# ScalarE writes the causal masks of two attention layers into the score banks, in place of TensorE's mask products

## The reference, cut to what matters

```python
# layer one: 16 heads, dense causal attention
s = (einsum('bqhd,bkhd->bhqk', qn, k_nope) + einsum('bqhr,bkr->bhqk', qr, k_rope)) * scale
s = where(key_idx[None, :] <= q_idx[:, None], s, NEG_INF)
p = softmax(s, axis=-1)
y = einsum('bhqk,bkhd->bqhd', p, v)
x = x + (y * silu(gate)) @ w_out

# layer two: 32 heads on 4 key heads, window of 128 keys, one sink logit for each head
diff = qi + BLOCK - kk                       # over the block before and the own block
valid = (diff >= 0) & (diff < 128) & (key_abs >= 0)
s = where(valid, s, NEG_INF)
m = maximum(max(s), sink)
e = exp(s - m)
p = e / (sum(e) + exp(sink - m))
x = x + (einsum(p, v) * silu(gate)) @ w_out

# then: the final norm of block one, a layer with block attention and a state-space mixer,
# and a gated feed-forward of width 5632 with a convolution of 3 taps
```

## Time and profile before

| | |
|---|---|
| median of 3 runs | 1928.05 us (1927.01 to 1928.12) |
| the profiled execution's own time | 1934.19 us |
| its span, first to last instruction | 1932.0 us |
| TensorE busy | 1839.2 us (95%) |
| TensorE weight loads busy | 1701.6 us (88%) |
| VectorE busy | 1109.4 us (57%) |
| ScalarE busy | 893.8 us (46%) |
| GpSimd busy | 151.6 us (8%) |
| mean granted clock of TensorE | 0.981 |

### The profile page before, as it was taken

How to read it: one execution, slowest core, us unless ns; L and a number is a source line. 1 busy time by engine, 2 the same in 40 slices (tenths; PEclk the granted TensorE clock), 3 DMA queues, 4 the chain that set the end, 5 groups by cost and what they waited for, 6 DMA issues and landing times.

```text
span 1932.0 us, 35128 instructions
## 1 busy us (share of the span) xinstructions
PE 1839.2 (95%) x13112; PEld 1701.6 (88%) x13112; DVE 1109.4 (57%) x1575; ACT 893.8 (46%) x1347; POOL 151.6 (8%) x177
## 2 busy tenths in 40 slices
PE   6999999889999997999999996999999999999997
PEld 5899998789989776999999786999999999988885
DVE  6555555545665655665555555566666656644444
ACT  5454454444445444454443445445544454433333
POOL 1001110000011100000000000010000000023322
PEclk9999999989999998999999997999999999999998
DMA  6555545635554454456555453666666666555553
GB/s 221 164 149 143 157 152 171 185 100 173 151 146 142 141 163 143 130 157 185 164 147 158 152 188 119 196 195 190 191 194 195 191 191 194 194 185 193 192 192 119
DMA packets 234789, 324.24 MB, mean 168 GB/s; under 512 B 12272, under 2 KB 170116, under 8 KB 234080
## 3 DMA queue, kind: packets, MB, share of 16 engines
q1 hardware_dynamic: 233296, 317.63, 53.6%
q0 software_dynamic: 1136, 4.58, 0.7%
q10 hardware_dynamic: 288, 1.09, 0.2%
HBM read 321.14 MB, written 2.11 MB: 167 GB/s over the span
## 4 chain that ended last, share of the span: by engine, by line
PE 89%; DVE 5%; ACT 3%; issue 2%; DMA 0%; POOL 0%; ACTq 0%; DVEq 0%
PE bank L481 16%; PE bank L482 16%; PE bank L483 16%; PE bank L489 7%; PE bank L491 7%; PE bank L490 7%; PE bank L516 3%; PE bank L1045 3%; PE bank L1046 3%; PE bank L1047 3%; PE scores L516 3%; PE bank L519 1%; PE scores L1046 1%; PE scores L1045 1%; PE scores L1047 1%
## 5 line engine op out<-in xcount | busy, mean ns | idle before, releaser
L1521 DVE TENSOR_TENSOR w_low<-raw,w_high 128x1024 fp32r<-128x1024 f32 x603 | 739.6, 1230 | 692.5 <-ACT w_high L1069 691.9
L1069 ACT CAST w_high<-raw 128x1024 fp32r<-128x1024 f32 x603 | 630.7, 1050 | 767.8 <-PE bank L483 419.9
L481 PE MATMUL bank<-hT_high,w_high 128*128 128x256 f32 x2672 | 751.0, 281 | 10.2 <-issue 3.2
L482 PE MATMUL bank<-hT_low,w_high 128*128 128x256 f32 x2672 | 743.4, 278 | 0.0
L483 PE MATMUL bank<-hT_high,w_low 128*128 128x256 f32 x2672 | 743.4, 278 | 0.0
L481 PEld LDWEIGHTS bank<-hT_high,w_high 128*128 128x128 f32 x2672 | 505.8, 189 | 16.0 <-issue 13.4
L482 PEld LDWEIGHTS bank<-hT_low,w_high 128*128 128x128 f32 x2672 | 505.2, 189 | 1.0 <-issue 1.0
L483 PEld LDWEIGHTS bank<-hT_high,w_low 128*128 128x128 f32 x2672 | 505.2, 189 | 0.0
L489 PE MATMUL bank<-w_high,yT_high 128*128 128x512 f32 x384 | 151.7, 395 | 2.1 <-POOL yT_low L2162 2.1
L491 PE MATMUL bank<-w_high,yT_low 128*128 128x512 f32 x384 | 150.5, 392 | 0.0
L490 PE MATMUL bank<-w_low,yT_high 128*128 128x512 f32 x384 | 150.3, 391 | 0.0
(11 more groups left out here) (270 smaller groups left out, 1961.3 us busy)
## 6 DMA issues: line engine op xcount, KB each, us to landing
raw<-in_w_up SPq DMA_DIRECT2D x176, 512.0 KB, 3.5
raw<-in_w_in SPq DMA_DIRECT2D x88, 512.0 KB, 3.7
raw<-in_w_down SPq DMA_DIRECT2D x88, 512.0 KB, 4.4
raw<-in_w_swa SPq DMA_DIRECT2D x72, 512.0 KB, 3.7
raw<-in_w_c SPq DMA_DIRECT2D x50, 512.0 KB, 3.8
raw<-in_w_mlao SPq DMA_DIRECT2D x32, 512.0 KB, 3.8
raw<-in_w_swao SPq DMA_DIRECT2D x32, 512.0 KB, 4.2
raw<-in_w_out SPq DMA_DIRECT2D x32, 512.0 KB, 3.7
```

The source lines that it names most:

```text
L481: nc.tensor.matmul(to, h, act_h[:, chunk, :], start=first, stop=False, skip_group_check=True)
L482: nc.tensor.matmul(to, h, act_l[:, chunk, :], start=False, stop=False, skip_group_check=True)
L1069: nc.scalar.copy(whi(tile, i, n), raw[s][:, :]).then_inc(high_made, 1)
L1521: v.tensor_tensor(wlo(tile, i, n), raw[s][:, :], whi(tile, i, n).bitcast(F32), ALU.subtract).then_inc(low_made, 1)
```

## The change

ScalarE gets a new operation `seed`: right behind the exponentials of a pair (in layer two behind the sink's exponential too) it waits for them and copies the mask band, three blocks of 128 columns for both heads, into the two score banks. The next pair's scores no longer start their banks anew but add onto it, and wait for the new semaphore `seeded` instead of the exponentials and `copy_pt1`. The mask products are gone, but for four: `seed_first` seeds the first pair of each layer by TensorE. The last pair of a layer is followed by no seed.

The flips can't lie in the score banks any more. In layer one their second half goes to bank 2, which waits for the keys' copy out of it (`k_out`); all flips stand one gate tile later, so the gate tiles are now split 1, 2, 1 around flips and values where they were 2, 2. In layer two four flips go to bank 6 and two into the half of bank 7 that the values leave free; `copy_pt0` takes 512 columns instead of 384 and `copy_pt1` 256 instead of 384, and the flips wait for `y32_done` of the pair before. In layer two's last step VectorE's `out_` moves in front of `norm`. GpSimd makes the middle block zero for layer one and copies the window's block there for layer two.

```diff
@@ -317,8 +317,9 @@
         ident_r = masks_r[:, 0, :]
-        mdiag_twice = masks_r[:, 1:2, :].to_broadcast([P, 2, P])
         mask_band = masks_r[:, 1:4, :]
+        band_of_both = masks_r[:, 1:4, :].bitcast(F32).rearrange("p b n -> p (b n)").unsqueeze(1).to_broadcast([P, 2, 384])
+        pT_row = pT[:, :, :].rearrange("p h n -> p (h n)")
         causal = cst[:, C_CAUSAL:C_CAUSAL + P]
@@ -553,6 +554,22 @@
+            def pair_transposed(st, p):
+                after(pe, st["p_ready"], p + 1)
+                after(pe, st["y32_done"], p)
+                after(pe, st["pt0_sb"], p)
+                after(pe, st["pt1_sb"], p)
+                for n in range(6):
+                    to = banks[6][:, n * P:(n + 1) * P] if n < 4 else banks[7][:, (n - 2) * P:(n - 1) * P]
+                    last = flip(to, prob[:, n // 3, n % 3 * P:(n % 3 + 1) * P])
+                last.then_inc(st["pt_ready"], 1)
+            def seed_first():
+                for h in range(2):
+                    f32mm(sc[:, h, 0:384], ident_r, mask_band, True, False)
@@ -608,15 +625,12 @@
                     after(pe, ml["k_out"], i)
-                    after(pe, ml["exp_done"], i - 1)
-                    after(pe, ml["pt1_sb"], i - 1)
+                    after(pe, ml["seeded"], i - 1)
                     for h in range(2):
...
                             to = sc[:, h, first:first + nk]
-                            f32mm(to, qn[:, h, q * P:(q + 1) * P], kn[:, h, 0:nk], q == 0, False)
-                            f32mm(to, qr[:, q * P:(q + 1) * P], krz[:, h, 0:nk], False, False)
-                        diagonal = sc[:, h, :].rearrange("p (q b n) -> p q b n", q=2, b=2)[:, :, 0, :]
-                        last = f32mm(diagonal, ident_r, mdiag_twice, False, True)
+                            f32mm(to, qn[:, h, q * P:(q + 1) * P], kn[:, h, 0:nk], False, False)
+                            last = f32mm(to, qr[:, q * P:(q + 1) * P], krz[:, h, 0:nk], False, True)
                     last.then_inc(ml["s_ready"], 1)
@@ -633,6 +647,7 @@
                     after(pe, ml["v_out"], i)
+                    after(pe, ml["pt1_sb"], i - 1)
                     for j in range(2):
@@ -655,20 +670,23 @@
                     after(pe, ml["y_split"], i - 1)
+                def gates(*js):
+                    if project and not gated_first:
+                        for j in js:
+                            tile_b(T_MLA + 4 + j, [banks[0][:, 0:SEQ], banks[0][:, SEQ:2 * SEQ]],
+                                   range(4 * j, 4 * j + 4), 256, hTh, hTl, 0, DC - 1, i, n)
                 out_tiles(0, 4)
+                gates(0)
                 if attend:
-                    probs_transposed(ml, i - 1, sc[:, 0, :])
-                if project and not gated_first:
-                    for j in range(2):
-                        tile_b(T_MLA + 4 + j, [banks[0][:, 0:SEQ], banks[0][:, SEQ:2 * SEQ]], range(4 * j, 4 * j + 4), 256,
-                               hTh, hTl, 0, DC - 1, i, n)
+                    after(pe, ml["k_out"], i + 1 if project else i)
+                    probs_transposed(ml, i - 1, banks[2])
                 out_tiles(4, 6)
+                gates(1, 2)
                 if attend:
                     weighted_values(ml, i - 1)
-                if project and not gated_first:
-                    for j in range(2, 4):
-                        tile_b(T_MLA + 4 + j, [banks[0][:, 0:SEQ], banks[0][:, SEQ:2 * SEQ]], range(4 * j, 4 * j + 4), 256,
-                               hTh, hTl, 0, DC - 1, i, n)
+                gates(3)
                 out_tiles(6, 8)
@@ -684,8 +702,9 @@
+            mla_step(0, True, False)
             pe.wait_ge(masks_made, 1)
-            mla_step(0, True, False)
+            seed_first()
             with pe.Fori(1, 8) as i:
@@ -715,20 +734,19 @@
             after(pe, sw["kz1"], 1)
+            pe.wait_ge(masks_made, 2)
+            seed_first()
...
                 after(pe, sw["q_placed"], i)
-                after(pe, sw["exp_done"], p)
-                after(pe, sw["pt1_sb"], p)
+                after(pe, sw["seeded"], p)
                 for first, q, nk in ((0, 0, P), (P, 1, SEQ)):
...
                         half = slice(64 * h, 64 * h + 64)
-                        f32mm(sc[:, h, first:first + nk], qs[half, m, q * P:(q + 1) * P], kz[half, i - 1, h, 0:nk],
-                              q == 0, False)
-                for h in range(2):
-                    last = f32mm(sc[:, h, 0:384], ident_r, mask_band, False, True)
+                        last = f32mm(sc[:, h, first:first + nk], qs[half, m, q * P:(q + 1) * P], kz[half, i - 1, h, 0:nk],
+                                     False, True)
                 last.then_inc(sw["s_ready"], 1)
@@ -771,7 +789,7 @@
                     if attend:
-                        probs_transposed(sw, 4 * (i - 1) + m, sc[:, 1, :])
+                        pair_transposed(sw, 4 * (i - 1) + m)
@@ -1126,10 +1144,15 @@
-            def copy_pt0(st, p):
+            def seed(st, p):
+                after(act, st["exp_done"], p + 1)
+                nc.scalar.copy(sc[:, :, 0:384], band_of_both).then_inc(st["seeded"], 1)
+            def copy_pt0(st, p, n=384):
                 after(act, st["pt_ready"], p + 1)
                 after(act, st["o_ready"], p)
-                nc.scalar.copy(pT[:, 0, :], banks[6][:, 0:384]).then_inc(st["pt0_sb"], 1)
+                nc.scalar.copy(pT_row[:, 0:n], banks[6][:, 0:n]).then_inc(st["pt0_sb"], 1)
@@ -1208,6 +1231,8 @@
                     exponentials(ml, i - 1, MLA_SCALE)
+                    if project:
+                        seed(ml, i - 1)
                 if not gated_first:
@@ -1266,10 +1291,12 @@
                         nc.scalar.activation(es[:, :, :], sd[:, :, :], ACT.Exp).then_inc(sw["sink_exp"], 1)
+                        if project or m < 3:
+                            seed(sw, p)
...
                     if attend:
-                        copy_pt0(sw, 4 * (i - 1) + m)
+                        copy_pt0(sw, 4 * (i - 1) + m, 512)
@@ -1573,7 +1600,7 @@
                 after(dve, st["o_ready"], p)
-                v.tensor_copy(pT[:, 1, :], src[:, 0:384]).then_inc(st["pt1_sb"], 1)
+                v.tensor_copy(pT_row[:, 768 - src.shape[1]:768], src).then_inc(st["pt1_sb"], 1)
@@ -1839,23 +1866,23 @@
                 tile(4)
+                out_(0)
                 norm(1)
                 tile(5)
-                out_(0)
                 pt1(1)
...
                 tile(7)
+                out_(1)
                 norm(2)
                 tile(8)
-                out_(1)
                 pt1(2)
...
                 tile(10)
+                out_(2)
                 norm(3)
                 tile(11)
-                out_(2)
                 pt1(3)
@@ -2163,7 +2190,8 @@
             g_.tensor_copy(masks_r[:, 0, :], ident)
-            g_.tensor_copy(masks_r[:, 1:3, :], cst[:, C_MDIAG:C_MDIAG + 2 * P])
+            g_.tensor_copy(masks_r[:, 1, :], mdiag)
+            g_.tensor_scalar(masks_r[:, 2, :], mprev, 0.0, None, ALU.mult)
             g_.tensor_copy(masks_r[:, 3, :], mdiag).then_inc(masks_made, 1)
@@ -2172,6 +2200,8 @@
             reciprocal_roots(2, 2, D, ss_done, 2, rstd_done)
+            after(pool, ml["s_ready"], 8)
+            g_.tensor_copy(masks_r[:, 2, :], mprev).then_inc(masks_made, 1)
             after(pool, sw["kz0"], 1)
...
```

More of the change, by code:

```diff
@@ L365, in program @@
                 "y32_done", "y_split")
-        ml = names("mla", *pair, "q_out", "k_out", "v_out", "rot", "q_rope", "tanh", "gate")
-        sw = names("swa", *pair, "q_out", "q_placed", "rot", "q_rope", "tanh", "gate", "vz", "sink_exp",
+        ml = names("mla", *pair, "seeded", "q_out", "k_out", "v_out", "rot", "q_rope", "tanh", "gate")
+        sw = names("swa", *pair, "seeded", "q_out", "q_placed", "rot", "q_rope", "tanh", "gate", "vz", "sink_exp",
                    "kv_out", "k_rot", "k_rope", "k_dup", "kz0", "kz1")
@@ L1056, in _ @@
         def _(act):
-            start(act, (ml, "exp_done pt0_sb q_out k_out tanh"),
-                  (sw, "exp_done pt0_sb q_out q_placed tanh sink_exp kv_out kz1"),
+            start(act, (ml, "exp_done seeded pt0_sb q_out k_out tanh"),
+                  (sw, "exp_done seeded pt0_sb q_out q_placed tanh sink_exp kv_out kz1"),
                   (mb, "exp_done pt0_sb q_out k_out v_out tanh"))
@@ L1701, in mla_step @@
                 if attend:
-                    copy_pt1(ml, i - 1, sc[:, 0, :])
+                    copy_pt1(ml, i - 1, banks[2][:, 0:384])
                 if gated_first:
@@ L1777, in pt1 @@
                     if attend:
-                        copy_pt1(sw, 4 * (i - 1) + m, sc[:, 1, :])
+                        copy_pt1(sw, 4 * (i - 1) + m, banks[7][:, 256:512])
                 def out_(m):
@@ L1993, in moba_step @@
                 if attend:
-                    copy_pt1(mb, i - 1, sc[:, 0, :])
+                    copy_pt1(mb, i - 1, sc[:, 0, 0:384])
                 if not project:
```

## The result

The changed kernel takes 1943.98 us (median of 5 runs, 1937.41 to 1948.85), the kernel before beside it 1928.12 (5 runs, 1927.01 to 1928.55): a ratio of 1.007, interval 1.0051 to 1.0089. The profiled execution is the slowest of the five, 1948.85 us, with a span of 1946.6 and a mean granted clock of 0.975, against 1932.0 and 0.981 before.

A forecast was written before the change was run, and what follows sets the result against it. TensorE was taken to bound layer one, the ScalarE-VectorE chain to the normalised `prob` layer two's last step. Terms -1.9 + 3.4 + 2.1 + 0.3 = +3.9 us gave 1931.9 us; 8-in-10 range 1926 to 1937.

The forecast's parts named there:

- The seed: ScalarE's mask copy into PSUM, between exponentials and next tile's copy: 0.81 us each, ends 0.5 and 1.1.
- The projecting steps: Layer two's three projecting steps: seeds delay m = 0 and 3, m = 1 and 2 gain; +0.7 a step, +2.1 us.
- The mask products: TensorE products removed: 0.12 us each in layer one, 0.50 for layer two's two, counting only where TensorE sets the pace.
- The 0.36: Layer two's two mask products at layer one's rate, right if a tiling-mode switch stays; sum 0.2 us higher.
- Layer one, -1.9 forecast: Layer one's attending steps: TensorE never waits, so removing mask products gains 8 x 0.24 = 1.9 us; seeds there cost 0.
- rival C: Layer one begins to wait, with the gate's product late for the next queries: +7 us on top, 1938.9 us; chance 0.13.
- Layer two's last step, +3.4 forecast: Three seeds on the chain, 2.4 us, plus gated output, 1.0; removed mask products gain nothing there.
- 3 x 0.33 = 1.0: Layer two's last step: gated output standing before the normalising in three pairs costs 0.33 us each.
- `seed_first`'s: TensorE seeding each layer's first pair: beside a wait in layer one, two products in layer two, +0.3 us.
- A: TensorE sets the pace everywhere and ScalarE's idle time takes the seeds: -9.6 us, 1918.4 us; chance 0.07.
- B: Not slower, because the seed is short: at 0.5 us a seed, +0.3 us, 1928.4 us; chance 0.15.
- D: The change doesn't do what it says, a seed overwritten or scores waiting for it; no chance given beyond C's.

The follow-up runs named there:

- e1: The changed kernel with the gated output behind the normalising again in layer two's last step; 1939.67 us, ratio 1.0051.
- e10: The kernel before with the mask products of both layers left out and nothing in their place; 1927.72 us, ratio 0.999.
- e4: The kernel before with only the gated output moved ahead of the normalising in layer two's last step; 1932.99 us, ratio 1.0014.
- e2: The changed kernel with unused 512-column products before layer two's flips, ten per last-step pair, five at m = 0 of projecting steps; 1939.51 us.
- e3: The changed kernel with each layer two seed one place later, behind the copy of the next tile's high part; 1929.72 us, ratio 1.0005.
- e7: The changed kernel with layer two as before, so layer one's part alone; 1927.68 us, ratio 0.9989.
- e8: e7 with layer one's gate product ahead of the last tile's low part; 1926.5 us, ratio 0.9985.
- e11: The kernel before with only layer one's gate product ahead of the last tile's low part; 1928.29 us, ratio 1.0001.
- e5: e3 with the last step's gated output right behind the maxima, ahead of the tile's low part; 1927.32 us, ratio 0.9985.
- e6: e5 with layer one's gate product ahead of the last tile's low part; 1926.28 us, ratio 0.9973.
- e9: e6 with five unused 512-column products ahead of each of the last step's four flips; 1926.64 us, ratio 0.9985.

## Why the prediction was wrong, point by point

*The seed.* Right in place and size: 0.80 us on the chain against 0.81. *The projecting steps.* Right in the mechanism; +2.1 forecast, +2.5 measured with the clock at 1.00 (e1), 4.0 in the profile of the changed kernel, whose first step alone is 60.66 us long against 59.37 and 59.32, at a clock of 0.94 in 473 to 501 us. *The mask products.* Layer one's 0.12 each is confirmed by e10. Layer two's two products give 0.55 (scores' start to values' start, 0.86 us against 1.41); I had taken 0.50. The 0.36 that I had put beside it by a rule of the Trainium skill (TensorEngine Tiling (Array Packing), Key Properties) did not come out: the values start 0.86 us behind the scores' start, where the mask products started before, and nothing of the 0.55 stays. Whether a change of tiling mode costs anything is not shown by this, since two changes (into the mask products and out of them) have become one.

*Layer one, -1.9 forecast, about -0.6 by the changed kernel's profile (seven steps of 0.08), and between 0.35 won and 0.26 lost in six steps by the five others with the same layer one.* The term failed by the mechanism of my rival C, at a quarter of its size: the gate's product comes late for the next step's first tile. I had written that TensorE never waits there and so the gain is whole, though I had the chain of C in hand. With the product early, the gain is there: 1.8 in six steps, where the mask products alone are 1.4 (e10).

*Layer two's last step, +3.4 forecast, +10.3 measured.* This is the step that failed, twice.

1. "From its start to the next operation's it is 0.33 us ... 3 x 0.33 = 1.0." It was 0.83 each, 2.5 in all (e4). I priced the gated output by VectorE's queue and did not ask what it releases: GpSimd's split moved with it, from beside a copy out of PSUM to beside the normalising, the last operations of the chain.
2. The sum has no term for the clock. I wrote that the waits grow "to some 2.5 us"; they grew to 3.5, which is 1.36 + 0.80 + 0.83 and the 0.54 of the mask products, which I had counted as worth nothing there and which TensorE now waits. Behind these waits the clock fell: 5.4 us in the profile, 4.5 in the median (e2). The kernel before has these waits at 1.36 us and a clock of 1.00, and I took that clock for given in a stage that I forecast to wait longer. The profile of before holds stretches at 0.75 and 0.82, behind the norms, that I did not read; a rival with the products behind a long wait at the lower level was missing. By what the profile shows now it would have been worth 1.6 and 2.5 us in the second and third pair (16.05 against e2's 14.48, and 16.22 against 13.70).

So the sum by the measured terms (the last, `seed_first`'s, is the forecast's own): -0.6 + 2.5 + 3 x 0.80 + 3 x 0.83 + 0.3 = +7.1, and with e2's 4.5 for the clock +11.6 of the measured 15.9. The remaining 4 us are not settled by an experiment. The profiles do close: of the 14.6 us between the spans the clock has 5.4 in the last step and 1.5 in the projecting steps (4.0 against e1's 2.5), and 7.1 + 6.9 = 14.0. But the profile of before is of an execution 6 us above its median. e2 says the same from the other side: its stages differ from those of before by 8 us, its median by 10.9. The profiles say where the rest can lie: from the norm's sum of squares behind layer two to the end, which no edit touched, it is 1172.4 us in the changed kernel, 1171.3 to 1172.9 in e1 and e2, and 1167.1 in e3, e7 and e8. The profiled execution of the kernel before has 1172.6, and that of e11, 7 us above its median too, 1172.7, so the profile of before hides such a difference. That the executions near the median of before have some 1167 there is likely by this and not shown, and what makes it longer is open.

*The rivals.* A (TensorE paces everywhere, 1918.4) is refuted by e10: with no masks and no seeds the time is still 1927.72, and the interval excludes the 9.6 us. B fell with the seed's size. D did not happen.

## What to carry to other kernels

Before taking work off the busiest engine, look for the stages in which it waits: there the work taken away becomes waiting, gives nothing, and the clock can fall. An instruction that is added to, or moved on, a chain is priced with everything that it releases on other engines, above all what VectorE and GpSimd then do at the same time. And a new operation off the critical path belongs behind the one that others wait for: the whole change cost 15.9 us with the seeds ahead of the next tile's copy and 1.1 with them behind it. With the two orders around them mended too it won 2.6, of which layer one's part alone has 2.3.

## What the runs showed of the hardware

- ScalarE writes 128 x 768 numbers into PSUM in 0.80 us, 0.74 from start to start; into SBUF it took 0.85 and 0.76. The TensorE products that follow, none of which starts a bank anew, add onto it, in 22 pairs.
- A normalising `TENSOR_SCALAR` of 128x128 takes 0.28 us alone and 0.74 beside GpSimd's subtraction; GpSimd's cast of 128x256 takes 0.40 alone and 1.23 behind VectorE's. I had not expected either to be visible.
- The length of TensorE's waits does not set the clock by itself. The five kernels that keep layer two's mask products (before, e4, e7, e8, e11) have 1.00 in 640 to 715 us of their profiles, e4 with waits of up to 2.24 us. Of the six without them and without added products in the waits, five fell (0.91 to 0.98; e3, e5, e6, e10 and the changed kernel), e5, e6 and e10 with waits of 1.9 us, and e1 did not, with waits of up to 3.1. Filled waits left it at 1.00 (e2, e9). Each kernel has one profile, so this is a pattern and not a rule. Ten products of 512 columns ahead of each wait, which nothing uses, gave back 5.4 us in the profile and 4.5 in the median.
- The single runs of the changed kernel follow the mean clock. They are 1948.85 us at 0.975, 1946.31 at 0.978, 1943.98 and 1943.07 at 0.980, and 1937.41 at 0.984. Part of this lies in stages that no edit touched, behind the norms; 1180 to 1215 us of the kernel before and of e7:

```profile
1180.00:1215.00 35.00, 26.25 (x184) 26.05 (x185) 17.84 (x32) 18.87 (x39) 1.53 (x3) 0.75 0.32 105
```

```profile
1180.00:1215.00 35.00, 29.91 (x246) 29.71 (x247) 18.85 (x30) 18.80 (x32) 1.33 (x2) 0.92 0.45 145
```

  The whole stretch behind layer two differs between the profiles by 5.8 us (1167.1 to 1172.9). That is why gains of 1 to 2 us, plain in the stages, are hard to see in the medians.
